# Head norms of keys and group norm: sums of squares by a block of ones on all partitions

## What is computed

```
kk = (k * k_k).reshape(B, S, H, N)
kk = kk / jnp.maximum(jnp.linalg.norm(kk, axis=-1, keepdims=True), 1e-12)
...
y = wkv7_scan(r_h, heads(decay), k_h, v_h, kk, heads(a))
mean = jnp.mean(y, axis=-1, keepdims=True)
var = jnp.mean(jnp.square(y - mean), axis=-1, keepdims=True)
y = ((y - mean) * lax.rsqrt(var + GN_EPS)).reshape(B, S, RW_WIDTH) * lnx_w + lnx_b
```

## Time and profile before

| | us |
|---|---|
| median of 3 runs | 883.03 |
| lowest and highest | 882.95, 885.43 |
| the profiled execution | 882.74 |
| its span, first to last instruction | 880.8 |
| TensorE busy in it | 853.7 |
| VectorE busy | 540.8 |
| ScalarE busy | 394.7 |

### The profile page before, as it was taken

How to read it: one execution, slowest core, us unless ns; L and a number is a source line. 1 busy time by engine, 2 the same in 40 slices (tenths; PEclk the granted TensorE clock), 3 DMA queues, 4 the chain that set the end, 5 groups by cost and what they waited for, 6 DMA issues and landing times.

```text
span 880.8 us, 16424 instructions
## 1 busy us (share of the span) xinstructions
PE 853.7 (97%) x7200; PEld 787.0 (89%) x7200; DVE 540.8 (61%) x592; ACT 394.7 (45%) x461; POOL 6.8 (1%) x8
## 2 busy tenths in 40 slices
PE   6999999999999999999999999999998999999997
PEld 6999889998988999999998989988887899999996
DVE  4898745445777765555556655477644665555664
ACT  6453331337356543343446344455535543333332
POOL 0000020000000000000000000000000000000000
PEclk9999999999999999999999999999999999999999
DMA  9745512231474646555653744426433365555541
GB/s 317 245 144 170 166 50 79 68 99 50 142 265 144 219 164 202 182 188 183 199 191 96 240 144 144 144 96 235 144 106 116 119 212 187 183 186 189 188 142 48
DMA packets 96715, 140.61 MB, mean 160 GB/s; under 512 B 2449, under 2 KB 79377, under 8 KB 96657
## 3 DMA queue, kind: packets, MB, share of 16 engines
q1 hardware_dynamic: 96368, 139.62, 48.7%
q10 hardware_dynamic: 288, 0.13, 0.1%
HBM read 138.69 MB, written 1.05 MB: 159 GB/s over the span
## 4 chain that ended last, share of the span: by engine, by line
PE 92%; DVE 3%; ACT 2%; issue 1%; DMA 1%; POOL 0%; POOLq 0%; SPq 0%; DVEq 0%; ACTq 0%
PE PS L393 90%; DVE wlo L1431 1%; PE PS L468 1%; DMA raw<-in_w_in_dram 1%; ACT st L1033 1%; ACT xh L1033 1%; ACT whi L1033 1%; DVE xl L1461 0%; PE PS L548 0%; PE PS L879 0%; POOLq L97 0%; DVE xn L1950 0%; POOL TT L1022 0%; POOL TT L1026 0%; DVE st L1622 0%
## 5 line engine op out<-in xcount | busy, mean ns | idle before, releaser
L1431 DVE TENSOR_TENSOR wlo<-raw,whi 128x2048 fp32r<-128x2048 f32 x125 | 285.7, 2291 | 153.5 <-ACT whi L1033 153.4
L393 PE MATMUL PS<-xh,whi 128*128 128x256 f32 x1136 | 326.8, 288 | 7.9 <-DVE xl L1461 7.7
L393 PE MATMUL PS<-xl,whi 128*128 128x256 f32 x1136 | 323.0, 284 | 0.0
L393 PE MATMUL PS<-xh,wlo 128*128 128x256 f32 x1136 | 323.0, 284 | 0.0
L1033 ACT ACTIVATE whi<-raw 128x2048 fp32r<-128x2048 f32 (+1 forms) x127 | 240.3, 1896 | 177.0 <-PE PS L393 163.8
L393 PEld LDWEIGHTS PS<-xh,whi 128*128 128x128 f32 x1136 | 219.5, 193 | 14.3 <-issue 8.4
L393 PEld LDWEIGHTS PS<-xl,whi 128*128 128x128 f32 x1136 | 219.6, 193 | 0.9
L393 PEld LDWEIGHTS PS<-xh,wlo 128*128 128x128 f32 x1136 | 219.5, 193 | 0.0
L393 PE MATMUL PS<-whi,fh 128*128 128x512 f32 x216 | 84.3, 391 | 0.0
L393 PE MATMUL PS<-wlo,fh 128*128 128x512 f32 x216 | 84.3, 390 | 0.0
L393 PE MATMUL PS<-whi,fl 128*128 128x512 f32 x216 | 84.0, 389 | 0.0
(11 more groups left out here) (303 smaller groups left out, 1056.5 us busy)
## 6 DMA issues: line engine op xcount, KB each, us to landing
raw<-in_w_in_dram SPq DMA_DIRECT2D x32, 1024.0 KB, 5.3
raw<-in_w_up_dram SPq DMA_DIRECT2D x16, 1024.0 KB, 5.4
raw<-in_w_down_dram SPq DMA_DIRECT2D x16, 1024.0 KB, 5.0
raw<-in_w_ffn_gate_dram SPq DMA_DIRECT2D x11, 1024.0 KB, 5.3
raw<-in_w_ffn_up_dram SPq DMA_DIRECT2D x11, 1024.0 KB, 5.4
raw<-in_w_ffn_down_dram SPq DMA_DIRECT2D x11, 1024.0 KB, 5.0
raw<-in_w_kv_mem_dram SPq DMA_DIRECT2D x8, 1024.0 KB, 5.4
raw<-in_w_o_dram SPq DMA_DIRECT2D x4, 1024.0 KB, 7.7
```

The source lines that it names most:

```text
L393: return nc.tensor.matmul(o, l, r, start=start, stop=stop, **kw)
L1431: V.tensor_tensor(wlo[u % RING][:], raw[u % RING][:], whi[u % RING][:].bitcast(f32), ALU.subtract) \
```

## The change

Both norms take their sums of squares with the constant block of ones (`blockones`, 128 x 128), as `y_sum` does: each head's sum then stands on all 64 partitions of that head. The root, the maximum and the reciprocal work on 128 partitions with the full length along the partition (1024 for the keys, 512 for a half of the group norm) and write into `kq` and `yq`, which has two buffers now. The four spread matmuls of each place, and their semaphores, are gone. The multiplication of `kk` stands right behind the reciprocal, and reads SBUF in place of PSUM.

```diff
                     for j in range(NPAIR):
-                        last = mm(PS[0:NH, 4 * 512:4 * 512 + SEQ], C("gather")[:, NH * j:NH * (j + 1)], kq[:, j, :], j == 0,
-                                  j == NPAIR - 1)
+                        last = mm(PS[:, 4 * 512 + j * SEQ:4 * 512 + (j + 1) * SEQ], C("blockones"), kq[:, j, :], True, True)
                     last.then_inc(sem("kk_ss"), 1)
...
                 by_feature(u, xh, xl, (i + 7) % 2)
-                if i == 0:
-
-                    pe.wait_ge(sem("kk_rs"), 1)
-                    for j in range(NPAIR):
-                        last = mm(PS[:, 4 * 512 + j * SEQ:4 * 512 + (j + 1) * SEQ], C("spread")[0:NH, j * P:(j + 1) * P], krs[:],
-                                  True, True)
-                    last.then_inc(sem("kk_spread"), 1)
...
-                    last = mm(PS[0:NH, (5 - tt) * 512:(5 - tt) * 512 + P], C("gather")[:, NH * j:NH * (j + 1)], yq[:, j, :], j == 0, j == NPAIR - 1)
+                    last = mm(PS[:, (5 - tt) * 512 + j * P:(5 - tt) * 512 + (j + 1) * P], C("blockones"), yq[tt][:, j, :], True, True)
...
                 if f == 1:
-                    y_spread(0)
                     y_squares(1)
-                if f == 2:
-                    y_spread(1)
...
-                    A_(krs[:], PS[0:NH, 4 * 512:4 * 512 + SEQ], ACT.Sqrt).then_inc(sem("kk_sd"), 1)
+                    A_(kq[:].rearrange("p j t -> p (j t)"), PS[:, 4 * 512:6 * 512], ACT.Sqrt).then_inc(sem("kk_sd"), 1)
...
-                A_(grs[:, tt * P:(tt + 1) * P], PS[0:NH, (5 - tt) * 512:(5 - tt) * 512 + P], ACT.Sqrt, scale=1.0 / HD,
-                   bias=small[0:NH, GEPS:GEPS + 1]).then_inc(sem("y_sd"), 1)
+                A_(yq[tt][:].rearrange("p j t -> p (j t)"), bank(5 - tt), ACT.Sqrt, scale=1.0 / HD, bias=col(GEPS)).then_inc(sem("y_sd"), 1)
...
                     dve.wait_ge(sem("kk_sd"), 1)
-                    link(V.tensor_scalar(krs[:], krs[:], 1e-12, None, ALU.max))
-                    V.reciprocal(krs[:], krs[:]).then_inc(sem("kk_rs"), 1)
+                    link(V.tensor_scalar(kq[:], kq[:], 1e-12, None, ALU.max))
+                    link(V.reciprocal(kq[:], kq[:]))
+                    V.tensor_tensor(kk[:], kk[:], kq[:], ALU.mult).then_inc(sem("kk_unit"), 1)
...
             queries(0)
-            dve.wait_ge(sem("kk_spread"), 1)
-            V.tensor_tensor(kk[:].rearrange("p j t -> p (j t)"), kk[:].rearrange("p j t -> p (j t)"), PS[:, 4 * 512:6 * 512],
-                                 ALU.mult).then_inc(sem("kk_unit"), 1)
             dve.wait_ge(sem("kk_unit"), 1)
...
-                V.reciprocal(grs[:, t], grs[:, t]).then_inc(sem("y_rs"), 1)
...
+                V.reciprocal(yq[tt][:], yq[tt][:]).then_inc(sem("y_rs"), 1)
```

More of the change, by code:

```diff
@@ L134, in block_kernel @@
         kq = at("kq", W + 66, [P, NPAIR, SEQ])
-        krs = at("krs", W + 94, [NH, SEQ])
         sq = at("sq", W + 70, [P, NPAIR, SEQ])
@@ L170, in block_kernel @@
         yc = at("yc", A0 + 8, [P, NPAIR, SEQ])
-        yq = at("yq", W + 42, [P, NPAIR, P])
+        yq = [at(f"yq{i}", W + 42 + 2 * i, [P, NPAIR, P]) for i in range(NT)]
         bon = at("bon", XR, [P, NPAIR, SEQ])
         rkk = at("rkk", W + 78, [P, NPAIR, SEQ])
-        grs = at("grs", W + 36, [NH, SEQ])
         rwoh = at("rwoh", W + 32, [P, NPAIR, SEQ], f32r)
@@ L1199, in y_square @@
                 act.wait_ge(sem("yc_ready"), tt + 1)
-                A_(yq[:], yc[:, :, tt * P:(tt + 1) * P], ACT.Square).then_inc(sem("y_sq"), 1)
+                A_(yq[tt][:], yc[:, :, tt * P:(tt + 1) * P], ACT.Square).then_inc(sem("y_sq"), 1)
             def y_root(tt):
                 act.wait_ge(sem("y_ss"), tt + 1)
-                A_(grs[:, tt * P:(tt + 1) * P], PS[0:NH, (5 - tt) * 512:(5 - tt) * 512 + P], ACT.Sqrt, scale=1.0 / HD,
-                   bias=small[0:NH, GEPS:GEPS + 1]).then_inc(sem("y_sd"), 1)
+                A_(yq[tt][:].rearrange("p j t -> p (j t)"), bank(5 - tt), ACT.Sqrt, scale=1.0 / HD, bias=col(GEPS)).then_inc(sem("y_sd"), 1)
             def y_round(tt):
@@ L1665, in y_inverse, with y_scale @@
                 dve.wait_ge(sem("y_sd"), tt + 1)
+                V.reciprocal(yq[tt][:], yq[tt][:]).then_inc(sem("y_rs"), 1)
+            def y_scale(tt):
+                dve.wait_ge(sem("y_rs"), tt + 1)
                 t = slice(tt * P, (tt + 1) * P)
-                V.reciprocal(grs[:, t], grs[:, t]).then_inc(sem("y_rs"), 1)
[L1669 to L1673, removed]
+                link(V.tensor_tensor(yc[:, :, t], yc[:, :, t], yq[tt][:], ALU.mult))
                 link(V.tensor_tensor(yc[:, :, t], yc[:, :, t], rw[:, 0:4, t], ALU.mult))
```

## The result

| | us |
|---|---|
| before, median (lowest to highest) | 883.12 (882.95 to 885.43) |
| changed, median | 894.03 (891.05 to 894.25) |
| ratio, with 95% interval | 1.011 (1.0083 to 1.0137) |
| profiled execution before: span | 880.8 |
| profiled execution changed: span | 892.2 |

The change makes the kernel 1.0 to 1.1% slower. The prediction was 889.9 us, with a range from 886.3 to 892.2. The direction held, and so did the mechanism at the two places of the change, but the first median lies above the range.

The account below looks back on a forecast made before the run. TensorE bounds the kernel, busy 853.7 of 880.8 us. Keys +3.4 and group norm +3.5 make 6.9 us on the profiled execution's 882.74, 889.6; with 0.3 for the median 889.9 us, range 886.3 to 892.2.

Parts of the forecast that it names:

- The spreads' 4.1 us: TensorE, both norms: dropping three spreads saves 1.92 us in the keys and two times 1.1 in the group norm.
- The fall behind the key spread: Old keys' part: clock at 0.50 from 67 to 71 us, put down to the 8-row spread; without it 1.8 us gained.
- The reciprocals: VectorE, both norms: time goes by length, 6.25 ns an element; keys 6.55 us, group norm 3.34 us, each of two.
- the estimate in the prediction: Reciprocals: repeat count of 8 read as cycles gives 8.3 ns an element, the sum some 2.5 us longer; not adopted.
- The keys' term: Second query unit: TensorE idle 5.35 us for the late evacuation, then low clock; +3.4 us, +1.9 without fall, +4.2 with long.
- I take the first: Keys, behind the wait: the low clock lasts 3.4 us (1.8 lost), chosen over 5 us (2.6 lost).
- The group norm's term: Second output product delayed by VectorE's chain: +2.6 us at least, +3.5 with a fall in the 2.95 us wait (taken), +4.4 if later.
- The sum: Whole program: 3.4 + 3.5 = 6.9 us on the profiled 882.74, plus 0.3 for the median, gives 889.9 us.
- I see no further wait: VectorE behind the keys: steps up to 6.5 us late, but pauses absorb it, so no further wait.
- the 1.7 us gap: Longest warm TensorE wait, in a stretch at clock 1.00; evidence for the rival without falls behind either gap: 887.5 us, chance 0.17.
- The range: Whole kernel: 886.3 to 892.2 us, said to take the first three cases and the dearer maximum.
- the cases: Whole kernel: forecast 889.9 us (0.54); no clock fall behind either gap 887.5 (0.17); longer or later falls 892.1 at most (0.16).

Follow-up runs that it names:

- ln and exp: Changed kernel with 1/sqrt by ScalarE as exp(-0.5 ln) for both norms, in place of root and reciprocal: 877.88 us, ratio 0.9942 to the kernel before.
- the run with the group norm alone: Kernel before with only the group norm changed and the keys' norm as before: 886.29 us, ratio 1.0044.
- changed again: The changed kernel run once more, unaltered, six runs: 891.1 us (890.3 to 894.55).
- The two runs of the keys alone: Kernel before with only the keys' norm changed and the group norm as before: 887.11 us (ratio 1.005), and again 887.82 us.
- the run with the order changed: Changed kernel with VectorE's group norm order as center 1, inverse 0, scale 0, inverse 1: 890.53 us.
- The filled wait: Changed kernel with unused TensorE products of the constant block, 24 in the keys' wait and 12 in the group norm's: 892.24 us; keys' 24 alone: 891.57.

## Why the prediction was right and wrong

- **TensorE's saving.** The spreads' 4.1 us are real. Stretches without a fall show it: from ScalarE's copy at 40 us to the one behind the second query unit it takes 30.5 us with ln and exp, and 32.9 with the old keys' part (the run with the group norm alone); in the group norm it is 14.55 against 17.15. That is 5.0 us. The new sums were a little cheaper too, by 0.3 us in the keys, where the forecast put nothing, and by 0.1 in the group norm, where it put 0.1 more.
- **The fall behind the key spread**, 1.8 us of the forecast's saving, is not a property of that spread: of four traces with the spread over 8 rows only the profile of before has a fall behind it. But the step was less wrong for the median than it looks. The kernel before has 47 single times in three groups: 14 near 881.2, 27 from 882.6 to 883.4, 6 near 885.5. Its profile, with this one fall, is in the middle group. Where the other executions of that group lose their 1.8 us no trace shows.
- **The reciprocals.** 6.55 and 3.35 us, forecast 6.55 and 3.34. The maximum took 0.69, forecast 0.67. Evacuation at 69.8 (69.9), restart at 70.55 (70.6), wait 5.64 (5.35, since TensorE got there 0.3 earlier). The trace gives 6.25 ns an element from 512 to 1024 too. The repeat count of 8 in the Trainium skill ("VectorE: DVE Perf Modes", section "First, the fixed hardware budget"), read as cycles, would have made the longer one 8.2 us by the estimate in the prediction; the trace decides against that reading.
- **The keys' term, forecast +3.4: measured +4.4 and +3.4**, each counted from ScalarE's copy ahead of the change, which by itself comes 0.1 us earlier in the first trace and 0.3 later in the second:

```profile
40.39 1.92 ACT L1033 ACTIVATE whi<-raw 128x2048 fp32r<-128x2048 f32 x1 [6.95 <-PE PS L393]
...
40.27 1.92 ACT L1013 ACTIVATE whi<-raw 128x2048 fp32r<-128x2048 f32 x1 [6.95 <-PE PS L391]
...
40.69 1.92 ACT L1013 ACTIVATE whi<-raw 128x2048 fp32r<-128x2048 f32 x1 [6.95 <-PE PS L391]
```

These are before, changed, and changed again. The two runs of the keys alone and the run with the order changed have this wait too: +3.6, +4.7 and +4.7. The step "I take the first" was the mis-sized one: it gave the fall 3.4 us, and all five falls lasted 6.8, of which 3.2 to 6.2 lay under the unit and the rest in the wait. That the repetition meets +3.4 is luck in where its fall lay.
- **The group norm's term, forecast +3.5: measured +2.6 and +3.5.** Both values stood in the prediction. Which one comes depends on whether the fall lies inside TensorE's wait or behind the sums. The filled wait, with neither, gave +2.6 as well.
- **The sum of the two places** is 6.9 and 7.2 in the two traces, forecast 6.9. In the first this is in part luck: the keys cost 0.9 more than forecast and the group norm 0.9 less.
- **The step that failed** is "The sum": it adds the two places to the profiled execution's time, and so puts the clock in all the rest of the program at no change, without a reason. The words "I see no further wait" held: no wait that is new outside the two places is over 0.5 us. Further falls came without one. They took 4.5 us of the first trace and 1.8 of the second, in passages that the change doesn't touch, and they come and go between executions of the same code: at 216 us in the changed kernel's first trace, not in its second; at 667 us in the keys' first trace, not in the second. The prediction had one of these passages before it: it took the 1.7 us gap that keeps 1.00 as a sign of no fall. In eight of the fourteen traces the clock falls at or within 1 us behind that gap.
- **The range.** The lower group of the changed kernel's times, 890.3 to 891.6, is in it; the upper, 894.0 to 894.6, is not. Mean clocks of 0.988 to 0.990 in the lower and 0.984 or 0.985 in the upper fit further falls, and the one traced execution of the upper group has them; the median of the first set lies in it. The range should have held at least two more falls of 1.7 us. Its lower edge, 886.3, follows from none of the cases, the lowest of which is 887.5.
- **What stays open.** The fall at 214 to 217 us was in five of the seven traces with the wide key reciprocal, and in none of the seven without it. Were the fall equally likely in all fourteen, five falls would all lie in that group about once in a hundred times (21 of 2002), so the change probably does make it more frequent, though the two groups were formed after the falls had been seen. By what is not shown. It isn't the shift alone, which brought none in at least three of four executions, and it isn't TensorE's idle time in the keys, since the fall came in both traces with that wait filled.

## What to carry to other kernels

A reciprocal on VectorE costs by its length along the partition, not by its partitions (8x256 and 128x256 both 1.75 us). To spread a value before root and reciprocal rather than behind them multiplies the dear reciprocal (6 ns an element) by as many pairs of heads as follow each other along the partition, here four. That is worth it only with a cheap way to 1/sqrt. Ask of every step made longer what is queued behind it on its engine: here an evacuation, for which TensorE stood still. And where times of one kernel form groups some 2 us apart, a single profile gives one member of a group; its clock falls belong in the range, not in the sum.

## What the hardware showed beyond what was expected

- The clock fell from 1.00 to 0.50 in a passage of small products whose longest wait was 0.6 us (216 us) and, in other executions of the same code, not. A fall there lasted 3.4 or 6.8 us and cost 1.4 to 2.8 us.
- The wait of 3.0 us for the second squares brought a fall in all four traces that have it, three times inside the wait and once a microsecond after its end; where it was filled there was none. With the order changed a wait of 2.8 us brought one too, worth 1.6 us.
- The kernel before has single times from 880.95 to 885.75 us, in groups at 881.2, 883.0 and 885.5; its mean clocks range from 0.998 to 0.990.
